# A hybrid mixer's retention branch: values transposed raw by TensorE and centered in VectorE's eviction, with the states and all behind them a quarter of a tile later

## The reference

```python
scores = einsum(qc, kc) * intra            # decay inside a chunk
inner = einsum(scores, vc)
cross = einsum(qc * q_dec, R)              # R: state of the chunks before
R = R * c_dec + einsum(kc * k_dec, vc)
...
mu = mean(o, axis=-1)                      # o = inner + cross, 128 channels of a head
var = mean(square(o - mu), axis=-1)
o = (o - mu) * rsqrt(var + EPS) * gn_g
return o * silu(zg)
```

## Time and profile before

| | |
|---|---|
| runs | 2050.01 us median of 3 (2049.46 to 2050.69) |
| profiled execution | 2050.12 us, its span 2048.3 us |
| TensorE | busy 99%, granted clock 0.998 of full |
| VectorE, ScalarE, GpSimd | busy 57%, 34%, 45% |
| a quarter of a tile on TensorE | 6 products, 1.38 us (1.4 to 1.5 behind small products) |
| `ahead` on ScalarE | 1.06 us |

### The profile page before, as it was taken

One profiled execution on the slowest core, in us unless ns is written; L12 is line 12 of the kernel. 1 busy time (PEld: TensorE's weight loads), 2 busy tenths in 40 slices (PEclk: granted clock), 3 DMA queues, 4 the chain that ended last, 5 costly groups with the idle time before them and its releaser, 6 DMA issues.

```text
span 2048.3 us, 31877 instructions
## 1 busy us (share of the span) xinstructions
PE 2021.5 (99%) x10036; PEld 1648.5 (80%) x10036; DVE 1160.9 (57%) x1727; ACT 686.9 (34%) x1029; POOL 918.5 (45%) x672
## 2 busy tenths in 40 slices
PE   8999999999999999999999999999999999999997
PEld 7777788888888888888887767888888888888886
DVE  7767755332227788862267677552232378888522
ACT  5365434233232222222234553332323232222222
POOL 3422234544445555555543223344444445554553
PEclk9999999999999999999999999999999999999999
DMA  6311132223222232223233112322323223323233
GB/s 213 114 53 42 62 99 83 92 92 102 95 99 93 93 97 97 96 95 109 94 129 101 53 42 78 93 83 93 101 92 102 93 86 101 101 92 102 97 103 111
DMA packets 58391, 193.36 MB, mean 94 GB/s; under 512 B 8000, under 2 KB 9536, under 8 KB 58176
## 3 DMA queue, kind: packets, MB, share of 16 engines
q1 hardware_dynamic: 52576, 186.17, 27.5%
q10 hardware_dynamic: 5728, 6.07, 1.2%
HBM read 185.13 MB, written 2.10 MB: 91 GB/s over the span
## 4 chain that ended last, share of the span: by engine, by line
PE 93%; DVE 3%; issue 2%; ACT 2%; DMA 0%; ACTq 0%; SPq 0%; DVEq 0%
PE acc L1247 29%; PE acc L1249 28%; PE acc L1248 28%; PE o L1462 2%; PE s L1432 2%; PE t L1443 1%; PE o L1520 0%; DMA w_raw<-weights_dram 0%; PE s L1500 0%; PE t L1483 0%; PE s L1549 0%; ACT pr_odd L578 0%; DVE pr L956 0%; ACT pr L578 0%; PE o L1523 0%
## 5 line engine op out<-in xcount | busy, mean ns | idle before, releaser
L446 POOL TENSOR_TENSOR w_lo<-w_raw,w_hi 128x512 fp32r<-128x512 f32 x668 | 918.3, 1396 | 1106.5 <-ACT w_hi L468 1090.6
L1247 PE MATMUL acc<-xg_hi,w_hi 128*128 128x512 f32 x1904 | 758.0, 398 | 5.7 <-DVE sc L757 1.8
L1249 PE MATMUL acc<-xg_hi,w_lo 128*128 128x512 f32 x1904 | 742.5, 390 | 0.0
L1248 PE MATMUL acc<-xg_lo,w_hi 128*128 128x512 f32 x1904 | 741.7, 390 | 0.0
L468 ACT ACTIVATE w_hi<-w_raw 128x1024 fp32r<-128x1024 f32 x336 | 355.4, 1058 | 771.2 <-PE acc L1249 746.3
L1247 PEld LDWEIGHTS acc<-xg_hi,w_hi 128*128 128x128 f32 x1904 | 357.5, 188 | 108.2 <-issue 32.2
L1249 PEld LDWEIGHTS acc<-xg_hi,w_lo 128*128 128x128 f32 x1904 | 357.4, 188 | 76.1
L1248 PEld LDWEIGHTS acc<-xg_lo,w_hi 128*128 128x128 f32 x1904 | 357.8, 188 | 72.0 <-issue 1.9
L1124 DVE TENSOR_TENSOR work<-acc,rstd 128x512 f32<-128x512 f32 x64 | 44.1, 690 | 256.1 <-PE acc L1249 256.1
L1247 PE MATMUL acc<-act_hi,w_hi 128*128 128x512 f32 x352 | 136.9, 389 | 0.0
L1248 PE MATMUL acc<-act_lo,w_hi 128*128 128x512 f32 x352 | 136.9, 389 | 0.0
(11 more groups left out here) (221 smaller groups left out, 2178.3 us busy)
## 6 DMA issues: line engine op xcount, KB each, us to landing
w_raw<-weights_dram SPq DMA_DIRECT2D x339, 512.0 KB, 3.3
x<-xT_dram SPq DMA_DIRECT2D x8, 256.0 KB, 6.1
rot<-rq ACTq DMA_DIRECT2D x16, 128.0 KB
rot<-rk ACTq DMA_DIRECT2D x16, 128.0 KB
out_dram<-x SPq DMA_DIRECT2D x8, 256.0 KB, 2.7
con<-consts_dram SPq DMA_DIRECT2D x1, 1406.0 KB, 10.4
w1k<-w_dram SPq DMA_DIRECT2D x2, 512.0 KB, 8.8
w1v<-w_dram SPq DMA_DIRECT2D x2, 512.0 KB, 7.3
```

What stands on the lines that cost most here:

```text
L446: nc.gpsimd.tensor_tensor(w_lo[:, slot, part], w_raw[:, slot, part], w_hi[:, slot, part].bitcast(F32), ALU.subtract).then_inc(lo_ready, 1)
L1247: mm(tile, w_h, right_hi, start=first, stop=False)
L1248: mm(tile, w_h, right_lo, start=False, stop=False)
L1249: return mm(tile, w_l, right_hi, start=False, stop=last)
```

## The change

TensorE's four products with `center` in `ret_turn` become four transposes by the identity; the matrix `center` is no longer made. VectorE, in place of ScalarE, evicts the turned values in three dependent instructions: it sums each position's 128 channels, multiplies the four sums per partition by the position's factor and -1/128, and writes value times factor plus that. ScalarE's copy of the keys now also waits for this eviction. The states, values, gate, variance, inverse, spread and end of each head move by one slot; the high half too, except for head 3, where it stays on slot 124, as the low half does on 126.

```diff
-    SIDE[_n0 + 2].append(("ret_state", _h))
-    SIDE[_n0 + 4].append(("ret_values", _h))
-    SIDE[_n0 + 5].append(("ret_gate", _h))
-    SIDE[_n0 + 6].append(("ret_var", _h))
-    SIDE[_n0 + 7].append(("ret_inverse", _h))
-    SIDE[_n0 + 8].append(("ret_spread", _h))
+    SIDE[_n0 + 3].append(("ret_state", _h))
+    SIDE[_n0 + 5].append(("ret_values", _h))
+    SIDE[_n0 + 6].append(("ret_gate", _h))
+    SIDE[_n0 + 7].append(("ret_var", _h))
+    SIDE[_n0 + 8].append(("ret_inverse", _h))
+    SIDE[_n0 + 9].append(("ret_spread", _h))
...
-    SIDE[RET_SLOT[_h] + (9, 9, 9, 9)[_h]].append(("ret_end", _h))
-    SIDE[RET_SLOT[_h] + (10, 10, 10, 11)[_h]].append(("ret_hi", _h))
-    SIDE[RET_SLOT[_h] + (11, 11, 11, 13)[_h]].append(("ret_split", _h))
+    SIDE[RET_SLOT[_h] + (10, 10, 10, 10)[_h]].append(("ret_end", _h))
+    SIDE[RET_SLOT[_h] + (11, 11, 11, 11)[_h]].append(("ret_hi", _h))
+    SIDE[RET_SLOT[_h] + (12, 12, 12, 13)[_h]].append(("ret_split", _h))
...
+        ret_mean = small[:, 106:106 + QT]
...
-                            elif e[0] == "ret_turn":
-                                act.wait_ge(t_done, t_use(L, e))
-                                act.wait_ge(dec_ready, L * 32 + 32)
-                                nc.scalar.activation(rv[:, :, :], t_of(e)[:, :].rearrange("p (k n) -> p k n", k=QT), ACT.Copy,
-                                                     scale=fall[:, e[1], 7:8]).then_inc(t_free, 1)
                             elif e[0] == "ret_keys":
                                 act.wait_ge(t_done, t_use(L, e))
+                                act.wait_ge(t_free, 1 + t_use(L, ("ret_turn", e[1])) + 1)
...
-                v_end(ve.scalar_tensor_tensor(out=center[:, :], in0=ones, scalar=-1.0 / RD, in1=ident, op0=ALU.mult, op1=ALU.add), "center")
...
                 def ret_turn(e):
+                    dve.wait_ge(dec_ready, L * 32 + 32)
+                    t_wait(e)
+                    src = t_of(e)[:, :].rearrange("p (k n) -> p k n", k=QT)
+                    col = fall[:, e[1], 7:8]
+                    then(ve.tensor_reduce(ret_mean, src, AX.X, ALU.add))
+                    then(ve.tensor_scalar(ret_mean, ret_mean, col, -1.0 / RD, ALU.mult, ALU.mult))
+                    t_end(ve.scalar_tensor_tensor(out=rv[:, :, :], in0=src, scalar=col, in1=ret_mean.unsqueeze(2).to_broadcast([P, QT, P]),
+                                                  op0=ALU.mult, op1=ALU.add), e)
...
                 def ret_turn(e):
                     pe.wait_ge(acc_free, 1 + L * TILES + (A_GROUPS + B_TILES.index(("rv", e[1])) + 2))
-                    if e[1] == 0:
-                        pe.wait_ge(v_made, v_count(L, "center"))
                     b = t_begin(e)
                     last_wait()
                     for k in range(QT):
-                        ins = mm(b[:, k * P:(k + 1) * P], rv_T[:, k * P:(k + 1) * P], center[:, :], start=True, stop=True)
+                        ins = nc.tensor.transpose(b[:, k * P:(k + 1) * P], rv_T[:, k * P:(k + 1) * P], ident)
```

More of the change, by code:

```diff
@@ L152 @@
 assert len(S_USES) % 2 == 0 and len(T_USES) % 2 == 0
-V_MADE = ["win_k", "k0_scaled", "k1_scaled", "win_v", "k0", "k1", "arg", "hid", "q0", "q1", "q2", "q3", "kc", "center"]
+V_MADE = ["win_k", "k0_scaled", "k1_scaled", "win_v", "k0", "k1", "arg", "hid", "q0", "q1", "q2", "q3", "kc"]
 A_MADE = ["hid", "gate"]
@@ L270, in build @@
         w2v = at("w2v", [P, DH], F32, R4 + 4 * QT * 3 * HEADS + 4 * 224)
-        center = at("center", [P, P], F32, R4 + 4 * QT * 3 * HEADS + 4 * 224 + 4 * DH)
         den = small[:, 64:72]
@@ L1015, in ret_turn, with ret_keys @@
                 def ret_turn(e):
+                    dve.wait_ge(dec_ready, L * 32 + 32)
[6 more added lines that the diff above has]
+                                                  op0=ALU.mult, op1=ALU.add), e)
+                def ret_keys(e):
                     made["t"] += 1
@@ L1095, in _ @@
                          "cmp_turn": cmp_turn, "cmp_scale": cmp_scale, "scale": scale, "ret_scores": ret_scores, "ret_mask": ret_mask,
-                         "ret_turn": ret_turn, "ret_keys": ret_turn, "ret_state": ret_state, "ret_gate": ret_gate,
+                         "ret_turn": ret_turn, "ret_keys": ret_keys, "ret_state": ret_state, "ret_gate": ret_gate,
                          "ret_inverse": ret_inverse, "ret_end": ret_end, "ret_split": ret_split, "pool": pool, "conv": conv, "mean": mean, "rotate": rotate_ret}
@@ L1639, in _ @@
             ins.then_inc(spread_ready, 1)
-CHAIN_LAYER, CHAIN_J, CHAIN_F, CHAIN_D = 175, 4, 15, 2
+CHAIN_LAYER, CHAIN_J, CHAIN_F, CHAIN_D = 183, 4, 15, 2
 def _constants():
```

## The result

The changed kernel takes 2056.14 us, median of 8 (2054.70 to 2057.74), against 2050.01 before (2049.29 to 2050.73): ratio 1.0029, 95% interval 1.002 to 1.0038. It is 0.3% slower, 4.1 us above the forecast and 1.1 above the top of its range. The profiled execution took 2057.06 us (span 2055.3, granted clock 0.995), 6.9 more than that of before.

A forecast was written before the change was run, and what follows sets the result against it. TensorE, busy 99% of the span, was taken as the bound. Terms -3.6 - 0.5 - 0.6 + 6.6 + 0 = +1.9 us on 2050.12 gave 2052.0 us, called no change; range 2047.5 to 2055.0.

The forecast's parts named there:

- Part 1: Turn on TensorE: four transposes replace four centering products, 0.45 us less in each of 8 turns, -3.6 us.
- Part 2: Making of the centering matrix on VectorE goes: layer 2's wait for the gates vanishes, -0.5 us, once.
- Part 3: Eviction moves to VectorE: hidden in heads 1 to 3; head 0's values held 1.1 us, 0.15 before.
- Part 4: Head 0 a quarter later: spread's wait of 1.23 us goes; with the longer hold -0.3 per layer, -0.6.
- Part 5: Heads 1 and 2 a quarter later: root behind ScalarE's partner copies, spread waits 1.66 us in four places, +6.6.
- rival 2: GpSimd's subtraction stretches VectorE's work between gate and inverse, delaying the spread: +3.8 us, 2055.8, slower; 12%.
- Head 3: No partner copies at the head of its next tile, so the spread is hidden by 0.25 us: 0 us.
- Rival 1: No new wait in heads 1 and 2, table loaded early or partner copies not blocking: 2045.4 us, faster; 12%.
- rivals 3 and 4: 3: turn doesn't get shorter, 2055.5 us, 5%. 4: head 0's values aren't held longer, 2050.4 us, 13%.

The follow-up runs named there:

- slots_only: Kernel before with only the slots moved by one, centering products and ScalarE's eviction kept: 2054.23 us, ratio 1.0018.
- inverse_first: Changed kernel with VectorE inverting the roots of heads 1 to 3 ahead of the next query's rotation: 2055.36 us, ratio 1.0025.
- partners_behind: Changed kernel with ScalarE issuing the next key tile's partner copies behind the root in heads 1 and 2: 2054.72 us, ratio 1.002.
- both_orders: Changed kernel with the edits of `inverse_first` and `partners_behind` together: 2047.40 us, ratio 0.9985.
- room_again: The kernel of `room` once more, in five rounds: 2044.01 us, ratio 0.9969.
- room: Changed kernel with only head 0's slots shifted and two other VectorE steps moved behind head 0's state updates: 2044.48 us, ratio 0.9969.

## Why the prediction was wrong

The mechanisms were found. Three steps failed, all in one direction: two terms were too small, and one cost stood in no term.

- **Part 1, the turn**: right, -0.45 in each of 8. **Part 2, the matrix**: right, 0.57 for 0.5. But the moved slots alone remove the same wait (`slots_only`), so it isn't shown that the matrix had to go for it.
- **Part 3, "a hold of 0.9 to 1.3. I take 1.1"**: the first term that failed; measured 1.74 (+0.64 per layer). The arrival of TensorE was right to 0.02 us after the turn. VectorE's list was too short: I placed the end of the second update 9.26 us behind the turn without stretching, and it came at 10.73. The stretched pooling step gives 1.07 of this; I had taken 0.85. The idle time of 0.33 ahead of the first update gives the next part, and the earlier trace rows shows it as 0.32: it is no slack that a longer list uses up, it moves along. The last 0.06 is the sum and eviction, 1.66 to the next start instead of 1.6.
- **Part 4, head 0's order**: right, -1.23, root done at V+5.96 (6.3 was forecast). With Part 3's error head 0 comes to +0.36 per layer instead of -0.3: 1.3 us in two layers.
- **Part 5, "A new wait of 1.66 us, in 2 heads and 2 layers: +6.6"**: place and number right, size 7.87. In head 1 ScalarE's chain was right: with the inverse ahead of the rotation (`inverse_first`) the spread loses 1.70. The rotation adds 0.18 in each layer. Part 5 said that the waiting inverse does not block VectorE since the rotation stands in front of it, and looked only at who waits behind; the rotation in front was rival 2's, priced as a delay on top. `partners_behind` shows that it gives a wait of 1.72 alone, and `both_orders` that only both edits remove it. The larger part of the miss, 0.4 in each layer, is head 2's: VectorE pauses 0.47 ahead of the tile's eviction, and no other engine released it. In the kernel before and in `slots_only` a pause of 0.47 stands ahead of another step (at 321.2 and 325.5 us), and in each trace where it shows it comes ahead of the 468th or 469th VectorE instruction, and in layer 2 at the same place in the layer's count. So it seems to go with the number of instructions, of which the new turn adds three per head, and not with the step; what makes it stays open.
- **Head 3**: right, no wait. The Trainium skill (SBUF — State Buffer, Who interferes with whom) calls the ports that VectorE and GpSimd share an exclusive lock; by it the pooling step that begins ahead of GpSimd stays whole. The trace agrees: it began at 350.38, 0.08 ahead of GpSimd, and took 0.69; in head 0 it began at 246.05, 0.08 behind GpSimd, and took 1.76.
- **The clock**, no term at all: +1.6 in the changed kernel, and about 2.2 for each of the longer standstills. The forecast priced a wait at its length. It is the cost that the prediction put at nothing without a reason.

From 2052.0: head 0 +1.3, waits +1.3, clock +1.6 make 2056.2; measured 2056.1. Without the clock it would have been 2054.6, inside the range; and since the result lies 1.1 above the range, each of the three misses is large enough to decide it. How often the clock fell in the executions without a profile isn't known: the eight times spread over 3.0 us (1.4 before), and the last 15 us alone differ by up to 0.9 us between traces.

Rival 1 (no wait) is refuted; rivals 3 and 4 too. Rival 2 is half right: its mechanism acts in head 1 (rotation's products 1.21 and 1.76 instead of twice 1.78) and costs 0.18 there and nothing in heads 2 and 3. That its total of 2055.8 came near is luck.

## What to carry to other kernels

Where an edit moves a dependent chain, list what each engine has in front of each link at the new place, and treat every one that ends late as a cause of its own: removing one of two equal delays shows next to nothing. On an engine that others wait for, idle time ahead of an instruction can move with it, as the 0.33 us did here, and must stay in the sum. And when the bounding engine is TensorE, a new standstill of two microseconds is priced with a possible fall of its clock behind it; those of 4.4 us and more had it each time here.

## What the runs showed of the hardware

- After a standstill of 1.90 us ahead of head 2's spread TensorE's granted clock fell from 2.4 to 1.2 GHz in layer 1, in the same place in three traces (two of the changed kernel, one of `inverse_first`), for about 3 us at a cost of 1.6. It did not fall behind the waits of equal length in layer 2 of the same traces, nor behind any of 1.72. Behind the four of 4.4 to 4.8 us it fell each time.
- The first 20 us are as mixed: the clock fell at a wait of 1.98 us in the changed kernel's profile (mean 0.51 from 9.0 to 12.5 us) and at one of 2.36 in `partners_behind`, and stayed up behind one of 2.02 in `room_again`. So near 2 us the length of the standstill alone doesn't decide; what else does was not found.
- In the last 8 to 13 us the clock is down in every trace, that of the kernel before included. By and large, the sooner it falls, the longer the end takes: it fell 5.3 us behind the start of TensorE's last wait of 2.4 us in the kernel before, with 13.8 us from there to the end, and 2.0 us behind it in `room`, with 14.7.
- VectorE's 128x512 products of two operands in SBUF took 1.76 and 1.21 us beside GpSimd's subtraction and 0.69 without it, while its evictions out of PSUM in the same stretches kept to 0.69.
- The sum of 128x512 out of PSUM over 128 channels took 0.68 us, as long as an eviction; the eviction that also scales and adds a broadcast mean took 0.75.
- A table switch was followed at once by its function: the root starts at 291.92, 0.01 behind the load of 290.63 to 291.91. The Trainium skill (ScalarE: Activation LUTs, What ACT_TABLE_LOAD costs) adds a drain of 1.38 behind the load of 1.28; the load agrees, the drain appears in none of these chains, neither behind the load nor ahead of it (in `partners_behind` the load of 289.02 starts 0.02 behind the instruction before it).
